# Value and output products in 512-column pairs of panels, each panel holding half of the channels

## What is computed

```python
h = rmsnorm(x, g_mix); proj = h @ w_in            # q, k, v of 20 heads, then 2048 gate columns
merged = gate_a * (o_dilated @ w_branch_a) + gate_b * (o_moba @ w_branch_b)
x = x + merged @ w_out
x = x + cross_attention(rmsnorm(x, g_cross), rmsnorm(mem, g_mem), w_q, w_kv, w_o)
x = x + peer(rmsnorm(x, g_ffn), ...)              # per token and head 16 of 16384 experts, gathered
return rmsnorm(x, g_final)
```

## Time and profile before

| | us |
|---|---|
| median of 3 runs | 957.85 (957.78 to 960.41) |
| profiled execution | 957.2 |
| its span, first to last instruction | 955.3 |
| PE busy in the span | 810.4 |
| DVE busy | 619.5 |
| ACT busy | 411.5 |

### The profile page before, as it was taken

The page is one execution under the profiler, slowest core; times in us unless marked ns, Lnnn a source line. Parts: engine busy times, 40 slices in busy tenths (PEclk is TensorE's granted clock), DMA queues, the critical chain, the costliest instruction groups (busy, mean ns, idle before and its releaser), DMA issues.

```text
span 955.3 us, 11577 instructions
## 1 busy us (share of the span) xinstructions
PE 810.4 (85%) x3620; PEld 506.7 (53%) x3620; DVE 619.5 (65%) x1442; ACT 411.5 (43%) x1008; POOL 359.5 (38%) x303
## 2 busy tenths in 40 slices
PE   5999999999998899998998777777777777777776
PEld 4999998799987445554553233222232222322232
DVE  5433676465568887778767666676666766665454
ACT  5544565444574544544534423244232442324243
POOL 0000066040004455656545444444444444444510
PEclk9999999999999999999999999999999999999999
DMA  6987533257417999999999999999999999999994
GB/s 241 263 226 208 177 132 132 89 222 267 153 45 290 424 420 420 421 421 421 421 421 422 422 421 420 423 422 421 422 421 422 422 422 421 422 421 421 422 423 199
DMA packets 48803, 324.88 MB, mean 340 GB/s; under 512 B 5508, under 2 KB 8824, under 8 KB 10104
## 3 DMA queue, kind: packets, MB, share of 16 engines
q0 software_dynamic: 36864, 268.45, 67.6%
q1 hardware_dynamic: 11752, 55.61, 17.3%
q10 hardware_dynamic: 144, 0.26, 0.1%
HBM read 322.77 MB, written 1.54 MB: 339 GB/s over the span
## 4 chain that ended last, share of the span: by engine, by line
DMA 47%; PE 39%; issue 5%; ACT 4%; DVE 3%; POOL 1%; DVEq 0%; SPq 0%; ACTq 0%; POOLq 0%
DMA late_ring<-in_experts,expert 44%; PE y L870 9%; PE ps L610 8%; PE ps L611 8%; PE ps L612 8%; DMA arena<-in_experts,expert 2%; ACT diag L1183 1%; POOL late_ring L1798 1%; PE ps L710 1%; PE ps L698 1%; ACT acts L1176 1%; DMA raw<-in_panels 1%; DVE w_lo L1314 1%; PE ps L688 1%; ACT w_hi L951 1%
## 5 line engine op out<-in xcount | busy, mean ns | idle before, releaser
L870 PE MATMUL y<-late_ring,diag 128*128 128x512 f32 x504 | 241.2, 614 | 63.5 <-ACT diag L1183 63.5
L870 PE MATMUL y<-arena,diag 128*128 128x512 f32 x504 | 239.5, 611 | 58.9 <-ACT diag L1183 58.9
L1678 DVE CUSTOM_DVE_ANT_0 arena<-arena 128x1024 f32<-128x1024 f32 x127 | 155.5, 1225 | 100.8 <-DMA arena<-in_experts,expert 100.6
L1678 DVE CUSTOM_DVE_ANT_0 late_ring<-late_ring,arena 128x1024 f32<-128x1024 f32 x129 | 158.0, 1225 | 89.3 <-DMA late_ring<-in_experts,expert 88.8
L1798 POOL DMA_INDIRECT late_ring<-in_experts,expert x129 | 155.0, 1202 | 161.3 <-PE y L870 135.4
L1798 POOL DMA_INDIRECT arena<-in_experts,expert x127 | 156.5, 1233 | 150.0 <-PE y L870 111.2
L870 PEld LDWEIGHTS y<-late_ring,diag 128*128 128x128 f32 x504 | 93.6, 194 | 200.9 <-ACT diag L1183 102.5
L870 PEld LDWEIGHTS y<-arena,diag 128*128 128x128 f32 x504 | 92.9, 193 | 193.4 <-ACT diag L1183 97.6
L1168 ACT ACTIVATE acts<-dots 128x2 f32<-128x2 f32 x126 | 25.6, 203 | 333.4 <-DVE dots L1678 333.3
L1314 DVE TENSOR_TENSOR w_lo<-raw,w_hi 128x2048 fp32r<-128x2048 f32 x40 | 93.5, 2339 | 75.9 <-ACT w_hi L951 75.9
L610 PE MATMUL ps<-h_hi,w_hi 128*128 128x256 f32 x400 | 116.8, 292 | 1.0 <-DVE h_lo L1346 1.0
(11 more groups left out here) (246 smaller groups left out, 990.0 us busy)
## 6 DMA issues: line engine op xcount, KB each, us to landing
raw<-in_panels SPq DMA_DIRECT2D x41, 1024.0 KB, 4.9
arena<-in_panels SPq DMA_DIRECT2D x5, 1024.0 KB, 6.9
arena<-line_scratch SPq DMA_DIRECT2D x8, 320.0 KB, 9.3
late_ring<-in_experts,expert POOLq DMA_INDIRECT x129, 31.7
arena<-in_experts,expert POOLq DMA_INDIRECT x127, 31.7
x<-in_x SPq DMA_DIRECT2D x2, 512.0 KB, 4.5
arena<-in_mem SPq DMA_DIRECT2D x1, 1024.0 KB, 7.1
out<-x SPq DMA_DIRECT2D x3, 256.0 KB, 7.2
```

The costliest lines, as they stand in the source:

```text
L870: mm = pe.matmul(y[:, t, half * 512:(half + 1) * 512], diag[:, s % DIAGS, :], row[:, at:at + 512], start=False, stop=False, skip_group_che ...
L1678: i = nc.vector.tensor_tensor_reduce(row, row, h_rows[:, t, :], 1.0, 0.0, ALU.mult, ALU.add, dots[:, s:s + 1])
```

## The change

Values of panels 2 and 5 are made as one product of 512 columns, and so are those of 13 and 14, and the output in two products of 512 columns (`out0` with `out1`, `out2` with `out3`). The first panel of a pair now holds channels 0 to 511 of all 512 columns, the second channels 512 to 1023. `wide_tokens` takes two PSUM banks, one for each token tile, and adds up four chunks from the first panel and four from the second into both. Panel `qkv5` is moved up in the list, in front of `qkv3` and `qkv4` (new line `QKV_ORDER`); panel `qkv8` stays as it was. Both panels of a pair count as in use until the pair's last product (`last_product_of_panel`). The copies and additions of the products take one token tile of 512 columns each. The total of bytes, panels and multiplications is the same.

```diff
+QKV_ORDER = [0, 1, 2, 5, 3, 4] + list(range(6, 15))
+WIDE = {5: (2, 0), 14: (13, 3 * 256)}
...
+            "qkv2": "values5_1", "qkv5": "values5_1", "qkv13": "values14_1", "qkv14": "values14_1",
+            "out0": "out0_1", "out1": "out0_1", "out2": "out1_1", "out3": "out1_1",
...
+            def wide_tokens(names, product, acts_t):
+
+                banks = [begin(f"{product}_{t}") for t in range(TILES)]
+                half = CHUNKS // 2
+                for i, name in enumerate(names):
+                    w = panel(name)
+                    for t in range(TILES):
+                        for k in range(half):
+                            mm = split_product(banks[t][:, 0:512],
+                                               cut(acts_t, slice(None), i * half + k, slice(t * P, (t + 1) * P)),
+                                               cut(w, slice(None), slice(k * 512, (k + 1) * 512)),
+                                               i == 0 and k == 0, i == 1 and k == half - 1)
+                        if i == 1:
+                            mm.then_inc(product_ready, 1)
...
-            all_taken("qkv14")
+            all_taken("values14_1")
...
-            for j in range(4):
-                tokens_by_channels(f"out{j}", o)
+            for i in range(2):
+                wide_tokens((f"out{2 * i}", f"out{2 * i + 1}"), f"out{i}", o)
...
-            for j in range(15):
+            for j in QKV_ORDER:
                 pace(f"qkv{j}")
                 if j == MEM_NORM_AT:
                     act.wait_ge(mem_loaded, 16)
                     squares("mem", mem_rows)
                     roots("mem")
+                if j in WIDE_FIRST:
+                    continue
+                if j in WIDE:
+                    for t in range(TILES):
+                        b = take(f"values{j}_{t}")
+                        took(nc.scalar.copy(vv[:, t, WIDE[j][1]:WIDE[j][1] + 512], b))
+                    continue
...
-            for j in range(4):
-                pace(f"out{j}")
-                b = take(f"out{j}")
-                xs = x[:, :, j * S:(j + 1) * S]
-                took(nc.vector.tensor_tensor(xs, xs, b.rearrange("p (t c) -> p t c", t=TILES), ALU.add))
+            for i in range(2):
+                pace(f"out{2 * i + 1}")
+                for t in range(TILES):
+                    b = take(f"out{i}_{t}")
+                    xs = x[:, t, i * 512:(i + 1) * 512]
+                    took(nc.vector.tensor_tensor(xs, xs, b, ALU.add))
```

More of the change, by code:

```diff
@@ L44 @@
 GATE_ORDER = [0, 1, 2, 5, 6, 7, 3, 4]
-PANELS = ([f"qkv{j}" for j in range(15)] + [f"gate{j}" for j in GATE_ORDER]
+QKV_ORDER = [0, 1, 2, 5, 3, 4] + list(range(6, 15))
+WIDE = {5: (2, 0), 14: (13, 3 * 256)}
+PANELS = ([f"qkv{j}" for j in QKV_ORDER] + [f"gate{j}" for j in GATE_ORDER]
           + ["branch_a", "branch_b0", "branch_b1", "kv0", "kv1"] + [f"out{j}" for j in range(4)] + ["kv2", "kv3"]
@@ L48 @@
           + [f"qpeer{j}" for j in range(PEER_HEADS)])
+WIDE_FIRST = [first for first, _ in WIDE.values()]
 RAW_RING = 2
@@ L166, in product_order @@
         add(f"turn_mix{c}", "both")
-    for j in range(15):
-        add(f"qkv{j}", "act")
+    for j in QKV_ORDER:
+        if j in WIDE:
+            add(f"values{j}_0", "act")
+            add(f"values{j}_1", "act")
+        elif j not in WIDE_FIRST:
+            add(f"qkv{j}", "act")
         if j == 0:
@@ L191, in product_order @@
     add("kv1", "act")
-    for j in range(4):
-        add(f"out{j}", "dve")
+    for i in range(2):
+        for t in range(TILES):
+            add(f"out{i}_{t}", "dve")
     add("kv2", "act")
@@ L663, in _ @@
             turn("mix", mix_xn)
-            for j in range(15):
-                if j in VALUE_PANELS:
+            for j in QKV_ORDER:
+                if j in WIDE:
+                    wide_tokens((f"qkv{WIDE[j][0]}", f"qkv{j}"), f"values{j}", h_pair)
+                elif j in WIDE_FIRST:
+                    continue
+                elif j in VALUE_PANELS:
                     tokens_by_channels(f"qkv{j}", h_pair)
@@ L1065, in _ @@
                 pace(f"out{j}")
-            act.wait_ge(taken["dve"], taken_count("out3"))
+            act.wait_ge(taken["dve"], taken_count("out1_1"))
             squares("cross", x)
@@ L1919, with halves @@
     kv = column_panels(a["w_kv_cross"][0])
+    narrow = column_panels(w_in)
+    def halves(w):
+        n = w.shape[1] // 512
+        return column_panels(w, 512).reshape(n, P, 2, PANEL).transpose(0, 2, 1, 3).reshape(2 * n, P, PANEL)
+    wide = {}
+    for last, (first, _) in WIDE.items():
+        two = halves(np.concatenate([w_in[:, j * 256:(j + 1) * 256] for j in (first, last)], axis=1))
+        wide[first], wide[last] = two[0], two[1]
     panels = np.ascontiguousarray(np.concatenate([
-        column_panels(w_in)[list(range(15)) + [15 + j for j in GATE_ORDER]], column_panels(a["w_branch_a"][0], D), column_panels(a["w_branch_b"][0], 512),
-        kv[:2], column_panels(a["w_out"][0]), kv[2:], column_panels(a["w_q_cross"][0]),
+        np.stack([wide[j] if j in wide else narrow[j] for j in QKV_ORDER]), narrow[[15 + j for j in GATE_ORDER]], column_panels(a["w_branch_a"][0], D), column_panels(a["w_branch_b"][0], 512),
+        kv[:2], halves(a["w_out"][0]), kv[2:], column_panels(a["w_q_cross"][0]),
         column_panels(a["w_o_cross"][0], 512),
```

## The result

The changed kernel takes 971.12 us in the median of four runs (965.75 to 972.02), the kernel before 958.2 on the same chip (957.78 to 960.41). The ratio is 1.0125, with a 95% interval of 1.010 to 1.015: 13 us slower. The forecast was 962.4 with a range up to 966.0, so the direction was right and the size was not. The profiled execution took 970.5 us against 957.2 before. One run of the kernel before beside the later experiments, 978.54 us at a mean granted clock of 0.85 where the others have 0.99, is left out of every ratio.

The account below looks back on a forecast made before the run. PE bounds the kernel up to 300 us, the DMA engines after. -2.6 + 0.5 + 2.5 + 4.2 = +4.6 us on the profiled 957.2 gives 961.8, or 962.4 for the median; range 959.6 to 966.0.

Parts of the forecast that it names:

- The saving: In the four pairs, fewer, longer matmuls, 512 columns every 0.227 us, save 0.64 us a pair, -2.6 us in all.
- Both joints: PE waits behind the last value products (+2.5 us) and behind the output products (+4.2 us), where its cover is thin.
- the second rival: One of the two PE waits, behind the values or behind the output, does not bind: 958.3 to 960 us, chance 0.17.
- I put +0.5: In the projection, later issue of qkv7's load behind the first pair costs PE +0.5 us, keeping 0 and 3.1 as limits.
- the empty queue: The load queue should be empty when qkv7's load is issued at about 44.2, which speaks for a low stall.
- the bound of 3.1: Projection stall if the full 4.3 us of later qkv7 issue meets 1.2 us of slack at qkv13: 3.1 us.
- the 8.5 that were free: qkv7's load, issued at about 44.2, must land by 52.7, within 8.5 us, or PE waits.
- joint 1: Last value product to first score: gate1's split and a second copy come ahead on ACT's queue, +2.5 us.
- joint 2: Output products to the transposes of cross_xn: kv3's split comes ahead of the last two additions, PE stalls +4.2 us.
- The first rival: Late panels starve PE in the projection by 1.5 to 3.1 us, or matmuls take 0.233: 963.5 to 966, chance 0.22.
- the poor matmul: In the pairs, a 512-column matmul starts every 0.233 us instead of 0.227, so the saving is only 1.3 us.

Follow-up runs that it names:

- e7_no_first_pair: Changed kernel without the pair of values 2 and 5, panels in the old order: 966.88 us, ratio 1.0103 to the kernel before.
- e8_mended: Changed kernel without the pair of values 2 and 5, with copies and additions moved ahead of splits at both joints: 957.35 us, ratio 0.9988 to before.
- e9_first_pair_alone: Kernel before with only the pair of values 2 and 5 and its order of panels: 960.73 us, ratio 1.0027 to before.
- e5_joint1: Changed kernel with the copies of values 13 and 14 ahead of the split of gate1's panel: median 965.03 us, ratio 1.0087 to before.
- e4_no_scratch_loads: Changed kernel without the eight bias loads from scratch, bias set to zero by GpSimd: 965.77 us in one run, against 958.9 before.
- e1_out_pairs: Kernel before with only the two output pairs, all values as before: 962.75 us, ratio 1.006 to before.
- f1_wait_2: Kernel before with one needless ACT copy ahead of the last copy of the projection: 962.99 us in one run, against 958.9.
- f2_wait_4: Kernel before with two needless ACT copies ahead of the last copy of the projection: 965.36 us in one run, against 958.9.
- e2_value_pairs: Kernel before with only the two value pairs, output as before: 967.33 us, ratio 1.0093 to before.
- e3_both_joints: Changed kernel, all four pairs kept, with copies and additions moved ahead of splits at both joints: 960.68 us, ratio 1.0037 to before.
- e6_joint2: Changed kernel with DVE adding each output pair ahead of the splits that wait for the pair's end: 966.5 us, ratio 1.0088 to before.
- g1_early_scratch: All pairs, both moves at the joints, and the first four scratch bias loads issued at once behind qkv6: 964.29 us, ratio 1.0062 to before.

## Why the prediction was wrong in size

**The saving** was right: -2.6 forecast, -2.5 measured. The gap rule of the Trainium skill's page "TensorE: Matmul & The Clock Gate" ("Back-to-back issue gap"), weighed there, would have made it 0.5; the rows decided rightly.

**Both joints** were right: +2.5 and +4.2 forecast, +2.44 and +4.28 measured. Each chain read from the order of ACT's and DVE's rows stood in the new trace instruction by instruction. So the second rival, that one joint does not bind, is out.

**The first failed step is "I put +0.5"**, for the late panels, with its reason, the empty queue. Measured are 4.61 us, above even the bound of 3.1. The issue of `qkv7` was forecast well (43.57, forecast 44.2), and the queue was empty: the DMA share from 41.0 to 43.5 is 0.01. It landed after 8.4 us, just inside the 8.5 that were free. For that landing in the kernel before the prediction says that it has no row, but the trace has one. The load issued at 39.90 is split here, 9.8 us later, and ACT had to wait for it:

```profile
49.68 1.90 ACT L951 CAST w_hi<-raw 128x2048 fp32r<-128x2048 f32 x1 [2.68 <-DMA raw<-in_panels]
```

The two `raw` buffers are a loop. A load is issued when its buffer has been split, 4.26 us after that split's CAST began (49.68 to 53.94 before). So two panels take 4.26 us and a landing. PE takes 11.52 for two panels. The loop keeps up only while a landing takes under 11.52 - 4.26 = 7.26 us. Beside the scratch loads, from a panel's issue to its CAST, the landings were 7.2 to 10.3 us before and 6.7 to 11.6 after. The median of 4.9 that the prediction compared with is that of all 41 panels, most of them without such a neighbour.

So the projection was already losing ground before the change. From CAST to CAST over six panels, where PE needs 34.56 us, and what PE took for its products up to that of `qkv13` over 5.76 a panel:

| profiled execution | CAST of `qkv7` | six panels later | length | PE over 5.76 a panel |
|---|---|---|---|---|
| before | 49.68 | 86.25 | 36.57 | 0.0 |
| `e7_no_first_pair` | 47.62 | 85.77 | 38.15 | 0.0 |
| `e8_mended` | 48.71 | 89.45 | 40.74 | 2.6 |
| changed | 51.98 | 91.12 | 39.14 | 4.6 |
| `e9_first_pair_alone` | 52.80 | 92.85 | 40.05 | 4.8 |
| `e5_joint1` | 49.94 | 84.91 | 34.97 | 0.1 |
| `e4_no_scratch_loads` | 49.78 | 80.29 | 30.51 | 0.0 |

The kernel before lost 2.0 us in the loop and had just enough lead for it: the parts of `qkv7` were ready at 53.91, 3.8 us ahead of its product at 57.73, and 1.8 us were left at `qkv13`. In the changed kernel they are ready at 56.20 for a product due at 56.33, which is a lead of 0.1, and the loop then loses 4.58. With every landing as long as in the trace of before, the parts of `qkv13` would be there at 43.57 + 9.78 + 36.57 + 4.23 = 94.15, for a product due at 39.05 + 51.84 = 90.89: by this estimate PE waits 3.3 us. So the prediction's bound of 3.1 was near what the rows of before give, and the choice of 0.5 had no row behind it; the other 1.3 us are the longer landings of this execution.

The pair takes the lead away, and the landings decide what that costs. In the six profiles with the old order (before, `e1_out_pairs`, `e7_no_first_pair`, `e8_mended`, `f1_wait_2`, `f2_wait_4`) the six panels take 36.6 to 41.1 us and PE loses 0 to 2.6 us. With the pair and the old scratch loads (changed, `e2_value_pairs`, `e3_both_joints`, `e6_joint2`, `e9_first_pair_alone`) they take 39.1 to 41.1 and it loses 4.6 to 6.2 (the 5.5 of `e3_both_joints` with its halved clock in it). Only `e5_joint1`, with the same order and the same late places as the changed kernel, came through in 34.97 and lost 0.1. The scratch loads make the landings long: in `e4_no_scratch_loads` those that ACT had to wait for took 4.7 to 7.3 us. Why landings vary by some 4 us from one execution to the next stays open. The timed runs of `e9_first_pair_alone` put the pair at 0.8 to 4.3 us (0.0008 to 0.0045 of 957.29).

**The second failed step is a term that the sum did not have**: both joints were priced as if a wait ended when the awaited thing is there, with PE at full clock behind it. Behind joint 1 the clock cost 3.15 us, behind joint 2 most of 0.71. Mended joints give both back: `e5_joint1` 3.16 at the first, `e6_joint2` the halved stretch behind the second. The page of the Trainium skill named above prices such a stretch in its "Terms" as its length times one minus the clock's share: 6.8 x 0.5 = 3.4 us. The rows give 3.15, so the trace agrees roughly. The forecast asked only how long PE waits and not at what clock it comes back. The trace of before had a sign of it, in the gathers, where PE had waited 1.89 us ahead of 327.82; a window of it:

```profile
328.90:332.10 3.20, 3.20 (x5) 1.25 (x4) 2.86 (x6) 3.15 (x5) 0.61 (x1) 0.50 1.02 425
```

**The sum with the measured terms**: -2.51 + 4.61 + 2.44 + 4.28 + 3.15 + 0.71 + 0.84 + 0.17 - 0.95 = +12.7, where +4.6 stood. The first rival had the right place (starved panels between `qkv7` and `qkv13`), with a price of 1.5 to 3.1 that was too low. Its upper end, 957.85 + 8.0, is no sum of its terms: 3.1 of stall makes 7.2, and with the poor matmul besides 8.5. That changes nothing in the outcome. The +0.84 in self-attention was not pursued. The start of the first product varied from 13.5 to 15.4 us among profiled executions of all these kernels, and -0.95 is within that.

**The saving is plain in the rows and hardly visible in the time**: with the joints in another order and the first pair undone, three pairs leave 1.2 us in the median (`e8_mended`), with an interval that reaches to no change. Three pairs at 0.64 are 1.9, less 0.1 and 0.75 at the joints, 1.1; the agreement is in part luck, since the median of eleven runs can't tell a few tenths and the profiled run had 2.6 us of waits for panels in it.

## What to carry to other kernels

Where a wide product holds two buffer places until its end, look at what stands on each engine's queue between the product's end and the thing that is awaited: moving two copies and two additions ahead of splits gave back 10 of 13 us. Slack against a loop of buffers is not a fixed reserve: compare the loop's period (issue to landing, and the work until the buffer is free) with the consumer's, using landings of the same stretch and not the median of the program. And price a wait of TensorE of some 3 us, as those measured here, as the wait plus what it then runs at half the clock.

## What was unexpected of the hardware

- The granted clock fell to 0.50 at each gap of 3.4 us and more that was looked at: 3.40 or 3.41 at joint 1 (changed, `e2_value_pairs`, `e4_no_scratch_loads`, `e6_joint2`, `e7_no_first_pair`), 4.49 there in `f2_wait_4`, 4.41 or 4.42 ahead of the transposes (changed, `e1_out_pairs`, `e4_no_scratch_loads`, `e5_joint1`, `e7_no_first_pair`), 3.44 and 4.01 in the projections of `e2_value_pairs` and `g1_early_scratch`. It stayed up behind the gaps of 0.95 to 1.07 at joint 1. Between them it was not settled by the gap's length: 2.72 at joint 1 of `f1_wait_2` and 2.10 in the projection of `e3_both_joints` brought it down for 3.4 us, 2.38 in that of `e9_first_pair_alone` and 2.69 in that of `e8_mended` did not. Nor did the length settle how long it stayed down: 4.41 ahead of the transposes brought 3.4 us in the changed kernel, 4.42 brought 6.8 in `e4_no_scratch_loads`; 3.40 at joint 1 brought 6.8 in the changed kernel, 3.41 brought 10.2 in `e2_value_pairs`.
- A load of 1 MB that has a median landing of 4.9 us took 6.7 to 11.6 us beside scratch loads of 320 KB, and 12.4 us behind four of them that had been issued 8.7 us before.
- `e5_joint1` took 958.24 to 968.78 us in four executions on one chip, where seventeen of the kernel before on the same chip lay between 955.68 and 960.25. Its buffer loop has almost no slack, but that this is the reason is not shown.
